# Two-layer hybrid decoder trunk on one core: attention units one slot later, one chain step in each unit's insertion, chunk products in parts

## The reference

```python
h = rmsnorm(x, norm_w)
proj = h @ w_in                                   # 1024 x 4160
y_rwkv = rwkv7_time_mix(...)  * silu(gate)        # recurrence over time, 4 heads of 64
y_conv = short_conv_mix(...)  * silu(gate)
y_moba = moba_attention(...)  * silu(gate)        # causal, T5 bias
y_ret  = retention_chunkwise(...) * silu(gate)
x = x + concatenate([y_rwkv, y_conv, y_moba, y_ret]) @ w_out
```

## Time and profile before

| | |
|---|---|
| median of 3 executions | 580.36 us (580.28 to 580.75) |
| the profiled execution | 581.02 us, of which its span (first to last instruction) 579.2 us |
| PE busy | 567.9 us, 98% of the span |
| DVE, ACT, POOL busy | 378.2, 277.8, 249.3 us |
| mean granted TensorE clock | 0.997 of full speed |

### The profile page before, as it was taken

One profiled execution on the slowest core, in us unless ns is written; L12 is line 12 of the kernel. 1 busy time (PEld: TensorE's weight loads), 2 busy tenths in 40 slices (PEclk: granted clock), 3 DMA queues, 4 the chain that ended last, 5 costly groups with the idle time before them and its releaser, 6 DMA issues. The chain is left out here.

```text
span 579.2 us, 12727 instructions
## 1 busy us (share of the span) xinstructions
PE 567.9 (98%) x5244; PEld 464.1 (80%) x5244; DVE 378.2 (65%) x636; ACT 277.8 (48%) x555; POOL 249.3 (43%) x197
## 2 busy tenths in 40 slices
PE   9999999999989999999999999999999999999995
PEld 7978888887777777888898788888887777788884
DVE  4999976581568557674543897947435974778163
ACT  6485231343573475534656743324356435735253
POOL 5846551044923323436335456402386313145340
PEclk9999999999999999999999999999999999999998
DMA  8556625056432121354535433332644121224513
GB/s 281 157 143 203 215 79 117 1 130 147 111 76 74 38 74 45 110 179 141 163 116 139 110 76 107 96 60 72 141 130 119 38 75 38 72 74 147 182 38 144
DMA packets 103373, 64.58 MB, mean 111 GB/s; under 512 B 29151, under 2 KB 94227, under 8 KB 103316
## 3 DMA queue, kind: packets, MB, share of 16 engines
q1 hardware_dynamic: 103316, 63.77, 39.1%
HBM read 55.61 MB, written 8.14 MB: 110 GB/s over the span
## 5 line engine op out<-in xcount | busy, mean ns | idle before, releaser
L703 POOL TENSOR_TENSOR w_lo<-w_raw,w_hi 128x512 fp32r<-128x512 f32 x156 | 216.5, 1408 | 286.3 <-ACT w_hi L1289 280.6
L769 PE MATMUL bank<-act_hi,w_hi 128*128 128x512 f32 x432 | 173.1, 401 | 0.0
L772 PE MATMUL bank<-act_lo,w_hi 128*128 128x512 f32 x432 | 168.5, 390 | 0.4 <-issue 0.4
L771 PE MATMUL bank<-act_hi,w_lo 128*128 128x512 f32 x416 | 162.3, 390 | 0.0
L1289 ACT ACTIVATE w_hi<-w_raw 128x512 fp32r<-128x512 f32 x140 | 80.2, 620 | 75.8 <-PE bank L854 28.2
L769 PEld LDWEIGHTS bank<-act_hi,w_hi 128*128 128x128 f32 x432 | 81.1, 188 | 24.7 <-issue 8.2
L772 PEld LDWEIGHTS bank<-act_lo,w_hi 128*128 128x128 f32 x432 | 81.1, 188 | 18.0 <-issue 0.8
L771 PEld LDWEIGHTS bank<-act_hi,w_lo 128*128 128x128 f32 x416 | 78.2, 188 | 14.8
L1215 PE MATMUL bank<-w_hi,act_hi 128*128 128x512 f32 x128 | 50.0, 390 | 0.0
L1217 PE MATMUL bank<-w_hi,act_lo 128*128 128x512 f32 x128 | 49.8, 389 | 0.0
L1216 PE MATMUL bank<-w_lo,act_hi 128*128 128x512 f32 x128 | 49.8, 389 | 0.0
(11 more groups left out here) (217 smaller groups left out, 948.2 us busy)
## 6 DMA issues: line engine op xcount, KB each, us to landing
w_raw<-in_w_in_dram SPq DMA_DIRECT2D x62, 512.0 KB, 4.0
w_raw<-in_w_out_dram SPq DMA_DIRECT2D x16, 512.0 KB, 3.8
pages<-in_x_dram SPq DMA_DIRECT2D x4, 512.0 KB, 6.0
x_or_y<-in_x_dram SPq DMA_DIRECT2D x4, 512.0 KB, 4.2
x_scratch<-x_or_y SPq DMA_DIRECT2D x4, 512.0 KB, 2.8
x_or_y<-x_scratch SPq DMA_DIRECT2D x4, 512.0 KB, 3.6
out_dram<-pages SPq DMA_DIRECT2D x8, 256.0 KB, 2.2
bias_scratch<-pages SPq DMA_DIRECT2D x1, 1280.0 KB, 7.5
```

The source lines that it names most:

```text
L703: ins = pool.tensor_tensor(low, raw, w_hi[:, i % HI, k, 0:n].bitcast(F32), ALU.subtract)
L769: mm(b[:, :], hi, act_hi[:, k, :], start=n == 0, stop=False)
L771: mm(b[:, :], lo, act_hi[:, k, :], start=False, stop=False)
L772: ins = mm(b[:, :], hi, act_lo[:, k, :], start=False, stop=n == KT - 1)
```

## The change

Six things are moved or cut. (1) The attention units stand one slot later: scores of unit u behind slot 12+2u, transposes in the middle of slot 14+2u. (2) The chain steps 1 to 6 stand one in each unit's insertion, just ahead of its scores. (3) `chunk_gh` computes h for the first of four time blocks alone, the other three follow as `chunk_h` behind the scores of unit 0, in other banks. (4) `chunk_y1` is cut by head pairs: one half behind the scores of unit 2, one behind those of unit 3; `chunk_q` and `queries` follow the scores of unit 1, `chunk_y` the values of unit 5. (5) The normalisation of RWKV's y moves: `ln_square` from slot 21 to 25, `ln_var` from 22 to 27, the reciprocals and scales from slots 22 to 27 to slots 27 to 30. (6) ScalarE makes the high part of the weight tile behind `mq1` after it has copied U and W, not before.

```diff
-                    (11, ("chunk_gh",)), (17, ("chunk_y1",)), (21, ("ln_square",)), (22, ("ln_var",))]:
+                    (11, ("chunk_gh",)), (25, ("ln_square",)), (27, ("ln_var",))]:
         mid[i].append(step)
-    for c in range(1, NCH - 1):
...
-        if c % 2:
-            mid[12 + c].insert(0, ("chain", c))
     after[9] += [("ret_root",), ("ret_recip", 0)]
...
-            mid[11 + 2 * u].append(("attend_turn", u - 1))
-            after[11 + 2 * u].append(("attend_values", u - 1))
+            mid[12 + 2 * u].append(("attend_turn", u - 1))
+            after[12 + 2 * u].append(("attend_values", u - 1))
...
-        if u in (1, 2, 3):
-            after[11 + 2 * u].append(("chain", 2 * u))
         if u < UNITS:
-            (after[11 + 2 * u] if u else mid[10]).append(("attend_scores", u))
-            (mid[12 + 2 * u] if u else after[11]).append(("attend_norm", u))
-    mid[15][1:1] = [("chunk_q",), ("queries",)]
-    after[19].append(("chunk_y",))
+            after[12 + 2 * u] += [("chain", u + 1), ("attend_scores", u)]
+            mid[13 + 2 * u].append(("attend_norm", u))
+    after[12].append(("chunk_h",))
+    after[14] += [("chunk_q",), ("queries",)]
+    after[16].append(("chunk_y1", 0))
+    after[18].append(("chunk_y1", 1))
+    after[24].append(("chunk_y",))
...
-                    (26, ("ln_scale", 0)), (27, ("ln_scale", 1)), (28, ("rwkv_finish", 0))]:
+                    (28, ("ln_scale", 0)), (30, ("ln_scale", 1)), (30, ("rwkv_finish", 0))]:
         after[i].append(step)
...
+        elif kind == "chunk_h":
+            layer += [("later0", 5, 1), ("later1", 6, 1)]
...
-                    by_chunk("g")
-                    by_chunk("h")
+                    by_chunk("g", "g", range(NT))
+                    by_chunk("h", "h", range(1))
+
+                def chunk_h():
+                    by_chunk("h", "later", range(1, NT))
...
+                def chunk_y1(p):
+                    by_chunk("y", "y", range(NT), (p,))
...
-                    else:
+                    elif job != "mq1":
                         weight_high(job, layer)
...
+                    weight_high("mq1", layer)
...
+                def decayed(job, t):
+
+                    we = w_end[:].rearrange("p a (t x) -> p a t x", x=2)
+                    for c in range(2):
+                        dve.wait_ge(*full(f"{job}{c}", layer))
+                        for p in range(2):
+                            ins = tt(par8(HP, c)[:, p, t], chunk_ps(f"{job}{c}")[:, p, t], we[:, p, t, c].unsqueeze(2).to_broadcast([P, t.stop - t.start, N]), ALU.mult)
+                        ins.then_inc(done(f"{job}{c}", layer), 1)
```

More of the change, by code:

```diff
@@ L296, in bank_jobs @@
             layer += [("g0", 5, 1), ("g1", 6, 1), ("h0", 7, 1), ("h1", 4, 1)]
+        elif kind == "chunk_h":
+            layer += [("later0", 5, 1), ("later1", 6, 1)]
         elif kind == "chunk_q":
             layer += [("q0", 6, 1), ("q1", 5, 1)]
-        elif kind == "chunk_y1":
+        elif kind == "chunk_y1" and step[1] == 0:
             layer += [("y0", 5, 1), ("y1", 6, 2)]
@@ L1069, in chunk_gh, with by_chunk @@
                         pe.wait_ge(*read(f"rows_kap{q}", layer))
-                    by_chunk("g")
-                    by_chunk("h")
+                    by_chunk("g", "g", range(NT))
+                    by_chunk("h", "h", range(1))
+                def chunk_h():
+                    by_chunk("h", "later", range(1, NT))
                 def chunk_q():
[L1074 to L1079, removed]
+                    by_chunk("q", "q", range(NT))
+                def chunk_y1(p):
+                    by_chunk("y", "y", range(NT), (p,))
+                def by_chunk(what, job, blocks, pairs=(0, 1)):
                     U, W = UW[:, :, 0, :], UW[:, :, 1, :]
-                    banks = [begin(f"{what}{c}", layer) for c in range(2)]
-                    for p in range(2):
-                        for t in range(NT):
+                    banks = [begin(f"{job}{c}", layer) if 0 in pairs else ps(f"{job}{c}", layer) for c in range(2)]
+                    for p in pairs:
+                        for t in blocks:
                             for hh in range(2):
@@ L1101, in by_chunk @@
                                         mm(o, U[r, m, :], SC[r, slot(t, h), 192:256], start=False, stop=t + c == 0, skip_group_check=True)
-                                    if p == 1 and t == NT - 1 and hh == 1 and what != "y":
-                                        end(ins, f"{what}{c}", layer)
+                                    if p == 1 and t == blocks[-1] and hh == 1 and what != "y":
+                                        end(ins, f"{job}{c}", layer)
                 def chain(c):
@@ L1897, in chunk_gh @@
                         ins.then_inc(done(f"g{c}", layer), 1)
[L1898 to L1902, removed]
+                    decayed("h", slice(0, 1))
                     for c in range(2):
@@ L1918, in chain @@
                     dve.wait_ge(*full(f"chain{c}", layer))
+                    if c == 2:
+                        for x in range(2):
+                            dve.wait_ge(*read(f"later{x}", layer))
                     b = ps(f"chain{c}", layer)
@@ L2051, in _ @@
                            attend_scores=attend_scores, attend_norm=attend_norm, attend_out=attend_out, conv_c=conv_c, conv_h=conv_h, conv_taps=conv_taps, conv_b=conv_b,
-                           conv_out=conv_out, chunk_gh=chunk_gh, queries=queries, chain=chain, chunk_y=chunk_y,
+                           conv_out=conv_out, chunk_gh=chunk_gh, chunk_h=chunk_h, queries=queries, chain=chain, chunk_y=chunk_y,
                            wide_out=wide_out, retain_sum=retain_sum, retain_scores=retain_scores, centre_v=centre_v, ret_stat=ret_stat, ret_recip=ret_recip, ret_finish=ret_finish,
```

9 lines of the change are left out of this document (5 added, 4 removed).

## The result

| | before | changed |
|---|---|---|
| median | 580.56 us (4 runs, 580.28 to 581.72) | 596.85 us (4 runs, 596.27 to 600.62) |
| profiled execution, span | 579.2 us | 594.5 us |
| mean granted clock of that execution | 0.997 | 0.989 |

The ratio is 1.0295, 95% interval 1.0271 to 1.032: 16.3 us slower. The direction and the main places were as forecast, the size was not: 588 was said, with 593 as the upper end.

What follows compares the result with a forecast made beforehand. TensorE, busy 98% of the span, was taken as the bound. 581.0 - 5.2 (gains) + 4.2 (attention waits) + 7.3 (layer end) + 1.5 (clock) = 588.8 us, given as a median of 588.0, range 582 to 593.

Steps and rivals of the forecast that it cites:

- Waits that go: Slot 11: TensorE's stops at g and h and layer 1's wait for U and W copies vanish, 3.4 us less.
- A cheaper list: TensorE's list: chain steps move to cheaper places and insertions are saved, 1.8 us less, bounds 0.6 and 2.8.
- The wait at the end of the layer: Ahead of `out` 0, TensorE is held for `split_y` of block 6, 3.65 us a layer, 7.3 us, bounds 6.6 and 9.3.
- Waits in the attention units: Units 0 and 1: TensorE waits for probabilities, 2.2 us without collisions, 6.2 with, entered at 4.2.
- The collisions: Units 0 and 1: second head's scalings on VectorE stand behind GpSimd's weight work, 1.0 us more each.
- In units 2 to 5: Later attention units: TensorE has as much cover as before or more, so no added wait.
- The clock: Behind each hold ahead of `out` 0, TensorE's clock falls, 0 to 1.8 us each, entered at 0.75, 1.5 in all.
- The range: Whole program: 582 to 593 us; terms at their upper ends gave 598, cut to 593.
- (a): Rival: layer's end is covered, TensorE isn't held and the clock stays, faster at 577.4 us; 13%.
- (c): Rival: clock stays low long after each hold in both layers, GpSimd collides at layer's end, 593 us or more; 10%.
- (b): Rival: TensorE's stops inside long runs come back elsewhere, gain shrinks to 3.2 us, 590.0 us; 10%.
- (d): Rival: gains and losses cancel, wait at the layer's end 1 us instead of 7.3, about 580.4 us; 5%.

Runs made afterwards that it cites:

- the last experiment: Kernel before with h in two parts plus the ScalarE edit: 577.44 us against 580.26, ratio 0.9955; set beside the best kernel, 576.88 us, ratio 0.9947.

## Why the prediction was wrong in size

**Waits that go, 3.4 us: right for the traced execution.** No idle is left in slot 11 of the changed kernel in either layer. The size belongs to one execution: the second trace of the kernel before has 2.6 us of such stops, and taking away both causes gave 2.6 us by the ratio. The cause given for the stops (PE's instructions too slow for 192 small ones on end) is consistent with h in parts ending them; that it is the supply of instructions was only argued.

**A cheaper list, 1.8 us: half of it, inside its bounds.** Gains came to 5.0 us by the account where 5.2 was said. Of these 3.4 are the waits above, and 0.7 are three small stops of the profiled kernel before (0.21, 0.15 and 0.36 us) that the change did not aim at. That leaves 0.9 us for this term, as the two kernels of the last experiment say too. That the sum of the gains came out so near is in part luck.

**The wait at the end of the layer, 7.3 us: right.** 3.53 us of idle in each layer, 7.4 us lost in all from product to product, by the chain of DVE and ACT as worked out; the late normalisation alone gave it in the kernel before.

**Waits in the attention units, 4.2 us: the first step that failed.** It measured 8.0. The part without collisions was said to be 1.1 us a layer and is 1.3, so that was right. The collisions were said to cost 1.0 us in each unit, and were entered at half of that, because their timing hung on a tenth of a microsecond. They came in both units and both layers, at 1.9 us in unit 0 and 0.8 us in unit 1. So 2.0 of the missing 3.8 us is the hedge, and the rest is mostly the price for unit 0. That price came from the earlier trace rows, where the first of the two scalings began at 453.52, ahead of POOL at 453.61, so that only the second stood. In the changed kernel both began behind POOL's start (177.16 against 176.96), and they ended behind both of its instructions. The prediction's own times had them so, the scalings at S + 6.3 and POOL at S + 5.8, yet it took the price of one instruction of POOL. The rule of the Trainium skill, page "SBUF — State Buffer", section "SBUF: two separate sides", of an exclusive lock held for a whole instruction, agrees with this: two scalings can stand for two instructions. The time alone does not show which of the two stood for which.

A small term was at nothing without a row: "In units 2 to 5" it said "nothing", and unit 5 waits 0.25 us in each layer for ACT's copies, 0.5 us in all.

**The clock, 1.5 us: the second step that failed.** It measured 4.4 in the profiled execution. Each hold was allowed 0 to 1.8 us, from the transposes at the start, and entered at 0.75; layer 0 cost 1.6 and layer 1 2.8, for there the low level outlasted the hold by 5.7 us. And the step looked at the two long holds only, where idles of 2.0 us can bring the clock down too, as the windows of the kernel with added matmuls show and the mean clocks of the slowest runs suggest.

**The range.** Summed at their bounds the terms reached 598 less 0.65, and 596.85 lies in that. The text cut it to 593 because all would have to fall badly together. That cut was wrong, and yet the full sum held the result only by luck: the attention waits (8.0) and the clock (4.4) both lay above their own upper bounds (6.2 and 3.6), and the wait at the end of the layer lay 1.9 us below its own. Beyond the profiled execution bad ends do meet, since a longer idle ahead of the transposes can also bring the clock down.

**Rivals.** (a) needed the tail covered; it took an edit to do that. (c), the clock low for long, is nearest to what happened. (b) and (d) did not.

## What to carry to other kernels

When an insertion is moved, follow the results of the slower engines to their next deadline on the engine that bounds, in their own order: a reader that waits for something in the middle of its queue (here the gate on a table load) delays all behind it. When a change adds an idle of some 2 us or more on TensorE, allow for what the lower clock may cost behind it (here between nothing and 2.8 us for each), and take the sum of the bad ends seriously, since the two go together. A part of a change that gains can be hidden by one that loses: here two small edits alone took 0.45% off the time, and the whole change added 2.95%. Before a collision is priced from a row, look how many instructions stood in that row: one here, where the changed kernel had two.

## What the runs showed of the hardware

- TensorE's granted clock fell to its lower level around an idle of 2.0 us in one execution and not in another with the same idle, nor in a third with an idle of 2.9 us. In the first it then stayed low for about 3.3 us. Behind the holds of 3.5 us it was low until 257.5 and 547.7, 3.1 and 5.7 us after PE had resumed. With filler matmuls in the hold it did not fall there.
- Two scalings of VectorE with operands in SBUF that began behind a pair of GpSimd instructions ended only behind both: 2.44 us against 0.55. The wait passed on to TensorE in full (1.9 us).
- PE stops of 0.3 to 1.8 us without a semaphore appear ahead of, inside or right behind the run of 192 small float32 matmul instructions of slot 11, in each of the four traces in which h was in one piece (the kernel before twice, late normalisation alone, the ACT edit alone), and in none of the ten in which it was in two. Stops of 0.2 to 0.5 us remain in other places in both kinds. Their cause is open.
